# TensorE takes the second tile's v rows during the mixer stages, and 24 v rows move into the second lane of the next phase

## The reference, cut to what matters

```
for l in range(DEPTH):                                   # DEPTH = 2
    mix = token_mixers(h, ...)       # A band attention, B recurrent block, C differential attention, gates, out projection
    h = layer_norm(ALPHA * h + mix)
    ff = peer_ffn(h, ...)
    h = layer_norm(ALPHA * h + ff)

# peer_ffn, for a block of 128 tokens xb
s = einsum('thpd,hpnd->thpn', xb @ w_q, sub_keys); sv, si = top_k(s, 16)
cand = sv[..., 0, :, None] + sv[..., 1, None, :];  fs, fi = top_k(cand, 16)    # 16 experts of 16384 a head
g = softmax(fs)
hid = gelu(einsum('td,thkd->thk', xb, u[experts]))
out = einsum('thk,thkd->td', g * hid, v[experts])
```

## Time and profile before

| | |
|---|---|
| time, median of 3 runs | 3902.18 us (3897.33 to 3907.54) |
| profiled execution, its own time and its span | 3898.55 us, 3896.7 us |
| VectorE busy | 2923.2 us, 75% of the span |
| TensorE busy | 2408.7 us, 62%, mean granted clock 0.807 |
| GpSimd busy | 2397.6 us, 62% |
| ScalarE busy | 531.2 us, 14% |
| DMA | 1295.78 MB, mean 333 GB/s |

### The profile page before, as it was taken

One profiled execution on the slowest core, in us unless ns is written; L12 is line 12 of the kernel. 1 busy time (PEld: TensorE's weight loads), 2 busy tenths in 40 slices (PEclk: granted clock), 3 DMA queues, 4 the chain that ended last, 5 costly groups with the idle time before them and its releaser, 6 DMA issues. The chain is left out here.

```text
span 3896.7 us, 29311 instructions
## 1 busy us (share of the span) xinstructions
PE 2408.7 (62%) x8928; PEld 1667.8 (43%) x8928; DVE 2923.2 (75%) x5647; ACT 531.2 (14%) x1237; POOL 2397.6 (62%) x2052
## 2 busy tenths in 40 slices
PE   8899527786798617767598717687788815600000
PEld 6676412464585313345486413355576513200000
DVE  2311786788877896778888797788777797798889
ACT  2310001122211101112110101122210101100000
POOL 0000377776675677766676577776566577777775
PEclk9989769997798859888698958998799968955555
DMA  4234699999899889999899989999799988999998
GB/s 176 96 107 140 213 324 361 369 392 348 294 408 409 339 316 347 368 384 392 325 389 409 352 321 347 361 390 391 291 365 409 370 323 308 355 350 367 368 387 339
DMA packets 359900, 1295.78 MB, mean 333 GB/s; under 512 B 40512, under 2 KB 40768, under 8 KB 359744
## 3 DMA queue, kind: packets, MB, share of 16 engines
q0 software_dynamic: 294912, 1073.87, 72.9%
q1 hardware_dynamic: 64256, 217.94, 14.8%
q10 hardware_dynamic: 576, 2.10, 0.1%
HBM read 1291.65 MB, written 2.10 MB: 332 GB/s over the span
## 5 line engine op out<-in xcount | busy, mean ns | idle before, releaser
L1057 POOL DMA_INDIRECT ring<-in_peer_u,eidx x1024 | 1222.6, 1194 | 960.1 <-DVE eidx L1181 475.1
L1057 POOL DMA_INDIRECT ring<-in_peer_v,eidx x1024 | 1174.8, 1147 | 516.8 <-issue 288.1
L1094 DVE CUSTOM_DVE_ANT_0 ring<-ring,hp 128x1024 f32<-128x1024 f32 x1024 | 1236.4, 1224 | 266.0 <-DMA ring<-in_peer_u,eidx 254.1
L1099 DVE SCALAR_TENSOR_TENSOR acc<-ring,wgt,acc 128x1024 f32<-128x1024 f32 x744 | 949.2, 1290 | 123.4 <-DMA ring<-in_peer_v,eidx 101.2
L519 PE MATMUL bank<-xt,panel 128*128 128x256 f32 x4096 | 952.8, 392 | 33.7 <-ACT raw L854 8.5
L519 PEld LDWEIGHTS bank<-xt,panel 128*128 128x128 f32 x4096 | 804.1, 198 | 164.0 <-issue 27.0
L752 PE MATMUL bank<-ring,dg 128*128 128x512 f32 x1120 | 549.6, 632 | 497.2 <-ACT dg L826 363.7
L752 PEld LDWEIGHTS bank<-ring,dg 128*128 128x128 f32 x1120 | 208.9, 198 | 825.4 <-issue 578.6
L594 PE MATMUL bank<-dg,ex 128*128 128x128 f32 x640 | 112.8, 349 | 149.2 <-DVE dg L1341 84.5
L594 PEld LDWEIGHTS bank<-dg,ex 128*128 128x128 f32 x640 | 105.4, 257 | 161.3 <-issue 145.7
L715 PE MATMUL bank<-yt,panel 128*128 128x256 f32 x768 | 173.6, 379 | 0.0
(11 more groups left out here) (164 smaller groups left out, 1884.0 us busy)
## 6 DMA issues: line engine op xcount, KB each, us to landing
panel<-in_panels SPq DMA_DIRECT2D x368, 512.0 KB
ring<-in_peer_u,eidx POOLq DMA_INDIRECT x1024
ring<-in_peer_v,eidx POOLq DMA_INDIRECT x1024
work<-in_rel_bias SPq DMA_DIRECT2D x16, 512.0 KB
gb<-in_ln_g SPq DMA_DIRECT2D x8, 512.0 KB
gb<-in_ln_b SPq DMA_DIRECT2D x8, 512.0 KB
panel<-in_keys SPq DMA_DIRECT2D x16, 256.0 KB
work<-in_x SPq DMA_DIRECT2D x4, 512.0 KB, 5.2
```

Of the source, the lines that this page charges most:

```text
L1057: pool.indirect_dma_start(ring[:, n % RING, :], None, t_in["peer_u" if kind == "U" else "peer_v"], bass.IndirectOffsetOnAxis(ap=eidx[:, t, ...
L1094: v.tensor_tensor_reduce(row, row, hp[:, t, :], 1.0, 0.0, ALU.mult, ALU.add, hid[:, t, c:c + 1]).then_inc(used, 1)
L1099: stt(out=acc[:, t, :], in0=row, scalar=wgt[:, t, c:c + 1], in1=acc[:, t, :], op0=ALU.mult, op1=ALU.add).then_inc(used, 1)
```

## The change

The row counts of the slots are changed: with 24 v rows (`BACK`) of a phase now standing in T1 of the next phase, stages A, C and G get 64, 60 and 76 rows in place of 76, 68 and 80; B (40), O, L, T0, T2, T3 and the 344 rows after the last phase keep theirs; T1 has 64 in place of 40. TensorE takes the second tile's v rows in A, B and C (14, 9 and 13 in a phase), and all 24 in T1. In T2 and T3 there are 28 v rows each, in place of 20 and 32. In all TensorE sums 476 rows, before 280. The second tile's sums stay in banks 6 and 7 from T2 of one phase to T1 of the next, so `weigh` has one bank, bank 1, which `outputs` writes too. The diagonals of the mixer stages lie in `work`, where `xn` was. `add_sums` and `finish` of the phase before move to after lane 1's choice. The wait for `added` at a phase's start moves from before the turn to before the first scores. C's v projection goes to banks 2 and 3.

```diff
 LAST = 2 * HEAD_ROWS
+BACK = 24
+AHEAD = 40
...
+def merged(a, b):
+
+    order = sorted([((2 * i + 1) * len(b), 0, i) for i in range(len(a))]
+                   + [((2 * i + 1) * len(a), 1, i) for i in range(len(b))])
+    return [(a, b)[j][i] for _, j, i in order]
...
+    rows, back = [], []
+    for p in range(PHASES):
+        u, v = u_rows(p), v_rows(p)
+        first = len(v) - LAST - BACK
+        rows += merged(back, u[:AHEAD]) + merged(v[:first], u[AHEAD:]) + v[first:first + LAST]
+        back = v[first + LAST:]
...
-LANE_ROWS = (0, 40, 64, 64)
-MIXER_ROWS = {"A": (16, 60), "B": (8, 32), "C": (12, 56), "G": (16, 64), "O": 16}
+LANE_ROWS = (0, AHEAD, 64, 64)
+MIXER_ROWS = {"A": (12, 52), "B": (8, 32), "C": (12, 48), "G": (12, 64), "O": 16}
...
-    return kind == "V" and stage == "T" and (it > 1 or it == 0 and k % 2 == 1)
+    if kind == "U":
+        return False
+    return stage == "T" and (it > 0 or k % 2 == 1) or stage in "ABC" and t == 1
...
-    return 2 * s + (it > 0) - 1
+    return 2 * s + (stage == "T" and it > 1) - 1
...
+def group_of(n):
+
+    p, kind, head, k, t = STREAM[n]
+    return (2 * (p + 1) - 1 if t else sum_group(n)), t
...
-        tp = bank[6:8]
+        tp = bank[1]
...
-                    if f < 2 and u:
-                        pe.wait_ge(pt_ev[kind], c - min(2, len(fills(s, kind))) + 1 if len(fills(s, kind)) > 1 else c)
-                    if f >= 2:
-                        pe.wait_ge(pt_ev[kind], c - 1)
+                    if f == 0 and u:
+                        pe.wait_ge(o_ev[kind], n)
+                    if f:
+                        pe.wait_ge(pt_ev[kind], c)
...
             def stage_a(s):
                 project_qk("A", s, 0)
+                sums((s, "A", -1, 1))
                 project_qk("A", s, 1)
+                sums((s, "A", -1, 2))
+                if s:
+                    pe.wait_ge(added, 2 * s - 1)
                 scores("A", s, 0)
-                project_v("A", s)
+                sums((s, "A", -1, 3))
+                pe.wait_ge(qk_ev["A"], s * UNITS + 2)
+                project_v("A", s, bank[0:2])
+                for i in range(4):
+                    sums((s, "A", 0, i))
                 for u in range(UNITS):
                     weigh("A", s, u)
                     if u + 1 < UNITS:
                         scores("A", s, u + 1)
+                    sums((s, "A", u, 4))
                     outputs("A", s, u)
+                    if u + 1 < UNITS:
+                        sums((s, "A", u + 1, 0))
+                        sums((s, "A", u + 1, 1))
                     if u + 2 < UNITS:
                         project_qk("A", s, u + 2)
+                    if u + 1 < UNITS:
+                        sums((s, "A", u + 1, 2))
+                        sums((s, "A", u + 1, 3))
...
-                    pe.wait_ge(added, 2 * s - 1)
                 turn(xn, bank[0:2], ready, x_turned, x_taken, s * 4)
...
-                    if it == 0 and s:
+                    if it == 1 and s:
                         add_sums(2 * s - 1)
                         finish(s - 1)
```

More of the change, by code:

```diff
@@ L127, in row_plan @@
                         plan += [((s, "B", j, i), k + (early if i + j == 0 else 0)) for i, k in enumerate(spread(n, 4))]
-                plan.append(((s, stage, -1, 0), before))
+                plan += [((s, stage, -1, i), k) for i, k in enumerate(spread(before, 4 if stage == "A" else 1))]
                 for u, n in enumerate(spread(total, UNITS)):
@@ L180, in rows_of, with last_in_lanes @@
     return range(lo, hi)
+def last_in_lanes(s):
+    return max(n for n in PE_SUMS if KEY_OF[n][:2] == (s, "T") and KEY_OF[n][2] == LANES - 1)
 class Own:
@@ L537, in project_qk @@
                 n = s * UNITS + u
-                if u:
+                b = bank[1] if kind == "C" and u == 1 else bank[0]
+                if kind == "C" and u == 1:
+                    pe.wait_ge(bg_ev, s * 2 + 1)
+                elif u:
                     pe.wait_ge(qk_ev[kind], n)
@@ L945, in stage_b @@
                         take_qk("C", s, 1)
+                take_v("C", s, bank[2:4])
             def stage_c(s):
@@ L1103, in add_sums @@
             def add_sums(group):
-                dve.wait_ge(pe_used, max(PE_PLACE[GROUP_ROWS[(group, t)][-1]] for t in range(TILES)) + 1)
+                tiles = [t for t in range(TILES) if (group, t) in GROUP_ROWS]
+                last = max(GROUP_ROWS[(group, t)][-1] for t in tiles)
+                if group % 2 == 0:
+                    last = max(last, last_in_lanes(group // 2))
+                dve.wait_ge(pe_used, PE_PLACE[last] + 1)
                 if last_sum:
                     dve.wait_ge(used, max(last_sum.values()) + 1)
-                for t in range(TILES):
+                for t in tiles:
                     for half in range(2):
@@ L1350, in attention_stage @@
                 else:
-                    rows((s, "A", -1, 0))
+                    for i in range(4):
+                        rows((s, "A", -1, i))
                 for u in range(UNITS):
@@ L1484, in _ @@
                 add_sums(2 * s)
+            add_sums(2 * PHASES - 1)
             for key in TAIL:
```

110 lines of the change are left out of this document (65 added, 45 removed).

## The result

The changed kernel is slower: 4013.73 us, median of 4 runs (3999.14 to 4024.44), against 3904.86 us (3897.33 to 3923.39) of the kernel before on the same chip. The ratio is 1.0269, 95% interval 1.0241 to 1.0296, or +105 us (the ratio is that of the means). The forecast had the sign, with +52 us; the time lies above its range.

The account below looks back on a forecast made before the run. VectorE was taken to bound C, TensorE to have little room in B and phase 3's A, and row issue to pace the lanes. Phases 1 and 3 at +25 us each and phase 2 at +2 gave +52: 3950 us, range 3855 to 4000.

Parts of the forecast that it names:

- The lanes: T1's 24 more gathers: +34 us, -7 for a vanishing VectorE wait, +3 for TensorE, so +30 us a phase.
- lower bound of +15: Lanes' smallest cost per phase, +15 us, if all three GpSimd waits in T1 and T2 give way.
- second rival: No change: the lanes take the gathers in at +15 us, giving 3906 us; chance 0.13.
- Head of the phase: Start of A: TensorE's 12 us wait for VectorE's add, moved behind the turn and two projections, counted as gain.
- A and B of the second halves: Phases 1 and 3: TensorE's added rows make A 13 us and B 8 us longer.
- the bank's 8 us: A of phases 1 and 3: single-bank fills waiting for ScalarE's copies cost 8 us, from a range of 6 to 10.
- C of the second halves: Phases 1 and 3: C starts 12 us late, then gets 16 us shorter, 5 of them from the clock.
- That absorbs about 9 of the 21 us: Start of C, phases 1 and 3: TensorE's 17.5 us wait for VectorE's rotary step takes in 9 us of delay.
- fit into its 55 us idle: C of phases 1 and 3: TensorE's 23 us of new rows go into its 55 us of idle time.
- Phase 2: The lighter phase: A -11, B +8, C -24 us, so -27 us in these stages.
- VectorE's relief: Rival: fewer VectorE rows in A, B, C outweigh the lanes, GpSimd issues perhaps gaining too: 3857 us; chance 0.32.
- The third: Rival: TensorE late in A and B of phases 1 and 3 holds ring buffers, unabsorbed at C: 4030 us; chance 0.12.

Follow-up runs that it names:

- e2: Changed kernel without the 24 v rows in T1 (BACK = 0, slot sizes of before), TensorE still summing in A, B and C: ratio to the kernel before 1.0299.
- e7: Kernel before with only the wait for `added` moved from before the turn to before the first scores: ratio 0.9973.
- e20: The kernel of e7 measured once more: ratio to the kernel before 0.9993.
- e11: Changed kernel with two weighing banks in A, one still in C: ratio to the kernel before 1.0266.
- e9: Changed kernel with the second tile's v rows of A, B and C gathered but nearly unsummed (VectorE takes 8 of 1024 columns): ratio to the kernel before 1.0042.
- e12: Changed kernel with TensorE's mixer rows in C only and two weighing banks in A: ratio to the kernel before 1.0008.
- e15: e11 with TensorE's products in A and B cut to 128 of 512 columns, C full: ratio to the kernel before 1.0157.
- e18: e12 without the 24 rows in T1 (BACK = 0, row counts of before): 3821.11 us against 3857.26 for the kernel before, ratio 0.9908.
- e10: Kernel before with only the new stream, slot sizes, T1's 24 TensorE rows and the later add and norm: ratio 1.0027.
- e19: The kernel of e18 measured again: 3824.63 us against 3850.53 for the kernel before, ratio 0.9918.
- e1: Changed kernel with all v rows of A, B and C back on VectorE, lanes and single bank kept: ratio to the kernel before 1.0194.
- e14: e6 plus an unused 256-column product after every fill but a unit's last: ratio to the kernel before 1.0062.
- e6: Kernel before with only the single weighing bank, each fill waiting for the copy of the one before: ratio 1.0129.

## Why the prediction was right in sign and short in size

**The lanes: right in number, in part by luck.** Forecast +30 a phase; measured +29, +32 and +28, between 20 and 38 in the other kernels with `BACK = 24`, and nothing in e2. From the first row issued for T1 to the first for T3, GpSimd takes 177 to 179 us before and 204 to 209 now, for 24 more rows. But the wait for VectorE, which was to give way (-7), grew from 6.8 us to 13 to 15 in every phase, while the wait for TensorE changed by -2 to +3 (forecast +3). T1 and T2 of phase 3:

```profile
POOL ring L1127 <- DVE hid L1163: 13.2, 2, 12.9
POOL ring L1127 <- PE bank L820: 7.0, 7, 3.1
```

What made up for it is the issue itself: its mean in T1 and T2 was 1.26 to 1.29 us before and is 1.11 to 1.16 now, over 128 issues a phase. The lower bound of +15 was a slip too: with all three waits gone (26 us) 34 leaves 8, and the second rival's price of 3906 would have been 3885.

**Head of the phase: wrong by 8 us.** "I take the 12 us as TensorE's gain." In e7 the first weighing comes 58 us after A's start and not 62, 4 us a phase; its ratio is worth 3 to 4 us a phase, and that of the same kernel in e20 (0.9993) under 1, within its noise. The step looked at the wait that ended, and not at what comes next. In the changed kernel the start of phase 3 on TensorE and on ScalarE reads:

```profile
2573.14 1.04 PE L562 MATMUL bank<-cst,work 128*128 128x128 f32 x8
2582.38 1.94 PE L562 MATMUL bank<-cst,work 128*128 128x128 f32 x8 [8.21 <-ACT xt L903]
```

```profile
2581.51 0.26 ACT L1072 ACTIVATE gate<-yt 128x64 f32<-128x64 f32 x1 [30.27 <-DVE yt L1264]
2581.67 1.05 ACT L903 COPY xt<-bank 128x512 f32<-128x512 f32 x2
```

TensorE turns eight blocks and stops, because ScalarE, whose copies free the two banks, stands behind lane 3's gates, and these wait for VectorE's choice. The turn had waited for the same choice before, through the add behind it.

**A and B of the second halves: right in the sum, by errors that cancel.** From A's start to the last weighing 139 us became 152 and 153, forecast +13; B +17 and +8, forecast +8. TensorE's three rows at 2629.49 in the trace took 5.31 us, 1.77 each, as forecast, and the bank's 8 us are near the 6 to 9 that e11 and the rows above show. Split by TensorE's own time, the forecast for head and A was 25 us more busy and 12 less idle; measured are 20 and 22 more busy, and 7 and 8 less idle. The head gave too little idle time back, and the clock (0.86 to 0.92 in the head, 0.93 to 1.00 behind it) took 3 to 4 us off the old products, for which the forecast had nothing.

**C of the second halves: the step that failed.** "That absorbs about 9 of the 21 us" and "I take 16 off C": 25 us forecast from B's end to the last weighing, against 6 and 2 (125 to 120 and 123). So A to C came out at +23 and +18 us where -4 was forecast. C of phase 3, before and in e9, where nobody does the rows:

```profile
2711.00:2836.00 125.00, 74.96 (x320) 60.41 (x320) 102.97 (x160) 24.13 (x65) 78.50 (x69) 0.71 0.84 315
```

```profile
2714.00:2823.00 109.00, 77.86 (x320) 61.06 (x320) 77.60 (x150) 24.22 (x65) 69.51 (x61) 0.70 0.87 326
```

Without the rows' work C does give 16 us. The step that failed is that TensorE's rows "fit into its 55 us idle". By these marks 50 us were idle. With 25 us off the length and 18 of new work (23 less 5 for the clock), 7 would be left; measured are 19 and 20, and 16 to 22 in C of the second halves of e11, e12, e15 and e18 too. And the rows were dearer there: their 55 records, four to a row, took 31 and 34 us, 2.3 to 2.4 us a row and not 1.76, since some ran at the lower level. One row in B and one in C of phase 3:

```profile
2783.56 1.88 PE L820 MATMUL bank<-ring,work 128*128 128x512 f32 x4
...
2812.48 3.75 PE L820 MATMUL bank<-ring,work 128*128 128x512 f32 x4 [4.15 <-DMA ring<-in_peer_v,eidx]
```

So TensorE's busy time in C grew by 26 and 28 us. Its clock rose from 0.71 to 0.80 and 0.79, but the old products only went from 75 to 72 us.

e10 shows a second double count: with 20 rows fewer and nothing on TensorE, C already falls from 125 to 111 and 116, and TensorE's rows add nothing to that (e12: 118 and 115, with the one bank). In the second halves either by itself takes 6 to 14 us off C (e10; e18 beside e20), and with both TensorE's rows give none; the rows without the lanes' part give 29 us in three phases (e19). The changed kernel kept even less, since it comes to C late and GpSimd waits 33.7 us for TensorE in C of phase 3.

**Phase 2: half right.** B +7 (forecast +8) and C -16 (-24) show the pattern, and head and A gave -4, not -11. The prediction's own sum did not close there: 89 + 25 + 3 is 117 us of TensorE, and 125 - 12 is 113. TensorE had room behind the head (47 us busy of 71 before, 61 of 70 after), but the rest of A did not shrink. In the windows the head runs at a DMA share of 0.74 (1.00 before) and the rest of A at 1.02. Head and A of e10, with the same rows, move as much in 120 us as the changed kernel in 134. So what GpSimd could not issue in the head was fetched behind it, with the DMA engines full; this is read from the windows, no run tests it.

**The account.** The forecast was +52; against it, A to C of the three phases cost 27, 14 and 22 us more, the tail 5 (505 to 510), G, O and the norm 4, and the lanes 1 less: +123, which is the growth of the span.

**The rivals.** VectorE's relief is real, 10 to 11 us a phase in C (e1 to e9), but as far as the runs show only if nobody else does the work; what spoke against it (PE's 110.9 of 126) held. GpSimd's issues did get shorter where VectorE was less busy: in T1 of phase 3 67.07/61 = 1.10 us at 71% (1.25 at 98% in the earlier trace rows); no run isolates a port. The third, TensorE late and holding ring buffers, described what happened in kind: no buffer free, 58.0 us of waits in A, no absorption at C. It had 0.12, and its price of 4030 us was nearer than the forecast's.

**The bank: right here, by a step that does not carry over.** 8 us in A of two phases was worked out from the length of a wait, and in the changed kernel A shows it (6 to 9 us). In the kernel before, the same bank costs 50 us, of which half comes back with the clock (e14); and the rest of A stays 8 to 11 us longer in every phase, in phase 2 too, where 3 were allowed. What the same stops do to the clock differs between the two kernels (A at 0.79 in e6, at 1.00 here), and the length of a wait does not tell that.

**What stays open:** why A and B together cost more than each alone; how much of the rows' cost is place and how much length, beyond e15's wide interval; what holds C of the second halves at 109 us once VectorE is relieved (e9), and at 111 to 123 with the rows on TensorE; and what a second bank in C would give.

## What to carry to other kernels

An engine busy for 65 of 71 us is full: new work there adds to the stage almost whole, and work behind it that holds shared buffers stops the engines that were meant to gain. Give a helper work only in the stages in which its own idle time is long (here C, where it was busy for 75 of 125 us), count as fillable only what the stage's chain of waits leaves (16 to 22 of the 50 us stayed idle here), and check that another edit has not already taken the same gain. When a wait is moved, follow the next step down to each engine that it needs, in that engine's own order.

## What was not expected of the hardware

Stops of 0.57 to 0.68 us after each fill took TensorE's granted clock in A from 0.93 to 0.79 and 0.86 in the second halves and from 0.81 to 0.63 in phase 2 (e6). All in all the single bank cost 50 us; filler products in the same stops brought back 0.94 in the second halves, and half of the time. Matmuls of useful rows between the steps had the same effect on the clock, with the stops left as they were (1.00 in the changed kernel, with the same single bank).
